# Gates and queries of the mLSTM heads: unscaled turned queries, and gate sums as scans, in a two-layer trunk step

## What is computed

```python
b = jnp.cumsum(fc, -1)
dmat = jnp.where(causal, b[..., :, None] - b[..., None, :] + ic[..., None, :], -jnp.inf)
inter = b + m[..., None]
m_out = jnp.maximum(inter, jnp.max(dmat, -1))
wmat = jnp.exp(dmat - m_out[..., None])
sw = jnp.einsum('bhtd,bhsd->bhts', qc, kc) * wmat
sc_in = jnp.exp(inter - m_out)
num = jnp.einsum('bhts,bhsd->bhtd', sw, vc) + sc_in[..., None] * jnp.einsum('bhvk,bhtk->bhtv', C, qc)
den = jnp.sum(sw, -1) + sc_in * jnp.einsum('bhk,bhtk->bht', n, qc)
h = num / jnp.maximum(jnp.abs(den), jnp.exp(-m_out))[..., None]
```

## Time and profile before

| what | value |
|---|---|
| median of 3 runs | 1513.45 us (1513.32 to 1513.97) |
| the profiled execution's own time | 1512.2 us |
| its span, first to last instruction | 1510.4 us |
| TensorE busy | 1393.6 us (92%) |
| VectorE busy | 622.0 us (41%) |
| ScalarE busy | 338.4 us (22%) |
| GpSimd busy | 340.0 us (23%) |
| mean granted TensorE clock | 0.972 |

### The profile page before, as it was taken

The page is one execution under the profiler, slowest core; times in us unless marked ns, Lnnn a source line. Parts: engine busy times, 40 slices in busy tenths (PEclk is TensorE's granted clock), DMA queues, the critical chain, the costliest instruction groups (busy, mean ns, idle before and its releaser), DMA issues.

```text
span 1510.4 us, 24451 instructions
## 1 busy us (share of the span) xinstructions
PE 1393.6 (92%) x9441; PEld 1071.4 (71%) x9441; DVE 622.0 (41%) x1473; ACT 338.4 (22%) x853; POOL 340.0 (23%) x455
## 2 busy tenths in 40 slices
PE   6999999898998999997899999989899889999964
PEld 5889899675887766564488899976678776656441
DVE  1121435677368312111353124548757852121117
ACT  1211211564101111110142121236431111111102
POOL 0100016632141311111010000744325221212101
PEclk9999999999998999999999999999799999999997
DMA  9420221765817999999732122256461599999984
GB/s 379 142 68 34 94 95 51 255 268 217 335 43 300 371 388 419 418 419 418 302 106 95 67 85 61 94 166 254 193 223 72 197 359 404 420 418 419 418 314 172
DMA packets 79714, 360.60 MB, mean 239 GB/s; under 512 B 20800, under 2 KB 24208, under 8 KB 46064
## 3 DMA queue, kind: packets, MB, share of 16 engines
q1 hardware_dynamic: 43632, 294.76, 49.4%
q0 software_dynamic: 19840, 44.63, 8.3%
q10 hardware_dynamic: 16128, 19.66, 4.1%
HBM read 346.49 MB, written 32.11 MB: 251 GB/s over the span
## 4 chain that ended last, share of the span: by engine, by line
PE 80%; DVE 8%; DMA 6%; issue 3%; ACT 1%; SPq 1%; ACTq 0%; DVEq 0%; POOLq 0%
PE bank L1159 22%; PE bank L1525 16%; PE bank L1396 8%; PE bank L1546 8%; DMA ring<-in_w_exp 4%; PE bank L965 2%; PE bank L1143 2%; PE bank L868 2%; PE bank L1322 2%; PE bank L1506 2%; PE bank L1296 2%; PE bank L1105 1%; PE bank L1418 1%; PE bank L1108 1%; DMA z<-expert_rows 1%
## 5 line engine op out<-in xcount | busy, mean ns | idle before, releaser
L1159 PE MATMUL bank<-ring,hT 128*128 128x256 f32 (+1 forms) x1600 | 338.8, 372 | 1.1 <-DVE z L2264 1.1
L1159 PEld LDWEIGHTS bank<-ring,hT 128*128 128x128 f32 x1600 | 291.9, 191 | 37.7 <-issue 1.6
L1525 PE MATMUL bank<-z,att 128*64 128x256 f32 (+2 forms) x960 | 176.8, 392 | 14.1 <-DMA ring<-in_w_exp 13.7
L1525 PEld LDWEIGHTS bank<-z,att 128*64 128x64 f32 (+2 forms) x960 | 117.3, 150 | 52.5 <-DMA ring<-in_w_exp 14.6
L1396 PE MATMUL bank<-ring,hT 128*128 128x256 f32 x640 | 141.9, 380 | 0.5 <-issue 0.5
L1396 PEld LDWEIGHTS bank<-ring,hT 128*128 128x128 f32 x640 | 120.1, 190 | 16.5 <-issue 0.7
L2717 DVE TENSOR_TENSOR att<-att,bank 128x256 f32<-128x256 f32 x36 | 15.2, 421 | 265.0 <-ACT att L1945 265.0
L3048 POOL DMA_INDIRECT expert_rows<-att,cur x36 | 37.0, 1029 | 354.0 <-DVE att L2730 341.4
L1525 PE MATMUL bank<-ring,att 128*64 128x256 f32 (+2 forms) x672 | 112.7, 398 | 1.8 <-ACT att L1938 1.8
L2264 DVE COPY z<-bank 128x512 f32<-128x512 f32 (+3 forms) x35 | 20.1, 578 | 173.6 <-PE bank L1159 173.6
L1525 PEld LDWEIGHTS bank<-ring,att 128*64 128x64 f32 (+2 forms) x672 | 69.7, 142 | 19.6 <-ACT att L1938 2.2
(11 more groups left out here) (401 smaller groups left out, 2316.7 us busy)
## 6 DMA issues: line engine op xcount, KB each, us to landing
z<-in_w_exp SPq DMA_DIRECT2D x74, 1024.0 KB, 21.9
ring<-in_w_exp SPq DMA_DIRECT2D x72, 1024.0 KB, 19.3
ring<-in_w_ada SPq DMA_DIRECT2D x41, 1024.0 KB, 6.4
ring<-in_w_in SPq DMA_DIRECT2D x24, 1024.0 KB, 5.0
hT<-in_w_exp SPq DMA_DIRECT2D x24, 1024.0 KB, 23.2
att<-in_w_exp SPq DMA_DIRECT2D x12, 1024.0 KB, 19.5
ring<-in_w_out SPq DMA_DIRECT2D x8, 1024.0 KB, 10.5
z<-expert_rows ACTq DMA_DIRECT2D x16, 512.0 KB, 8.6
```

What stands on the lines that cost most here:

```text
L1159: last = eng.matmul(bk[:, i * UN:i * UN + nw], hTv[:, k, t * P:(t + 1) * P], w[:, k, 0:nw], start=(k == 0), stop=(k == KD - 1))
L1525: last = eng.matmul(bank[2 + j][c * m_:(c + 1) * m_, u * DE:(u + 1) * DE], rows, wv[c][k // 4][:, k % 4, :], start=(k == 0), stop=(k == KD ...
```

## The change

TensorE no longer sums the forget gates: it turns input gates and forget gates, two transposes for each tile in place of three matmuls, and VectorE sums the turned rows with two scans for each tile, a backward one over reversed columns. The scaled and turned queries (`qs`, `qts`) are gone, with their transposes, VectorE's scaling and ScalarE's copies. Instead every latent tile keeps its turned, unscaled queries (`qT`, four tiles; tile 0 stays in `qkT`). In `step_values` TensorE writes weights x values to one bank (AN) and queries x state to another (AI), each a group of its own; VectorE multiplies the second with `gs` into `both`, adds the first, and goes on from `both` in SBUF. The job AI was there before (the transposes' bank, opened at g = 0); it is now opened at g = 1 between AN and AU.

```diff
-        a["qs"] = region(att, dead, P, 2, HA, DA)
-        a["qts"] = region(att, dead + 2 * D_A, DA, 2, HA, P)
+        a["qT"] = region(att, dead, DA, NT - 1, HA, P)
+        a["both"] = region(att, dead + (NT - 1) * HA * P, P, HA, W97)
+        turned_q = lambda t: qkT[:, 0] if t == 0 else a["qT"][:, t - 1]
...
-                        eng.matmul(bk[0:36, 0:P], a["gi"][:, t, :], ident, start=True, stop=True)
-                        eng.matmul(bk[0:36, P:2 * P], a["gf"][:, t, :], K["upper"], start=True, stop=False)
-                        last = eng.matmul(bk[0:36, P:2 * P], a["gbk"][:, t, :], K["lower"], start=False, stop=True)
+                        eng.transpose(bk[0:36, 0:P], a["gi"][:, t, :], ident)
+                        last = eng.transpose(bk[0:36, P:2 * P], a["gf"][:, t, :], ident)
...
-                def step_weights(si):
-                    for d, t in STEPS[si] if si > 0 else ():
-                        bk = jobs.open("AI", l, d, t)
-                        eng.wait_ge(*jobs.room())
-                        eng.wait_ge(*ev.at("qs", l, d, t))
-                        for h in range(HA):
-                            last = eng.transpose(bk[0:DA, h * P:(h + 1) * P], a["qs"][:, d, h, :], ident)
-                        last.then_inc(*jobs.filled())
...
-                                              start=True, stop=(t == 0))
-                            if t > 0:
-                                last = eng.matmul(bk[:, h * W97:(h + 1) * W97], a["qts"][:, d, h, :],
-                                                  a["CT"][:, d, h, :], start=False, stop=True)
+                                              start=True, stop=True)
                         last.then_inc(*jobs.filled())
+                        if si > 0:
+                            bk = jobs.open("AI", l, d, t)
+                            eng.wait_ge(*jobs.room())
+                            if si == 1:
+                                eng.wait_ge(*jobs.empty("AS", l, d))
+                                eng.wait_ge(*jobs.empty("AQ", l, t))
+                            else:
+                                eng.wait_ge(*ev.at("CT", l, d, t))
+                            for h in range(HA):
+                                last = eng.matmul(bk[:, h * W97:(h + 1) * W97], turned_q(t)[:, h, :], a["CT"][:, d, h, :],
+                                                  start=True, stop=True)
+                            last.then_inc(*jobs.filled())
...
-                def turned_queries(si):
-                    for d, t in STEPS[si] if si > 0 else ():
-                        bk = jobs.bank("AI", l, d, t)
-                        eng.wait_ge(*jobs.full("AI", l, d, t))
-                        eng.activation(a["qts"][:, d, :, :], bk[0:DA, :].rearrange("p (h n) -> p h n", h=HA),
-                                       ACT.Copy).then_inc(*jobs.freed("AI", l, d, t))
...
+                        for d in range(2):
+                            rows = a["brow"][32 * d:32 * d + HA, t * P:(t + 1) * P]
+                            rows = rows if d == 0 else rows[:, ::-1]
+                            last = eng.tensor_tensor_scan(rows, K["ones"][32 * d:32 * d + HA, 0:P], rows, 0.0, ALU.mult, ALU.add)
+                        last.then_inc(*dve.step())
+                        eng.wait_ge(*dve.last())
...
-                def scaled_queries(si):
-                    eng.wait_ge(*jobs.empty("AE", l))
-                    for d, t in STEPS[si]:
-                        if si > 1:
-                            pd, pt = STEPS[si - 1][d]
-                            eng.wait_ge(*jobs.full("AI", l, pd, pt))
-                        eng.tensor_tensor(a["qs"][:, d, :, :], h4(zv[:, t, C_QA:C_QA + D_A]),
-                                          bc(a["gs"][:, t, 32 * d:32 * d + HA], 2, DA), ALU.mult).then_inc(*dve.event("qs", l, d, t))
...
+                        if si > 0:
+                            state = jobs.bank("AI", l, d, t)
+                            eng.wait_ge(*jobs.full("AI", l, d, t))
+                            eng.wait_ge(*jobs.empty("AE", l))
+                            both = a["both"]
+                            eng.tensor_tensor(both, state[:, 0:HA * W97].rearrange("p (h n) -> p h n", h=HA),
+                                              bc(a["gs"][:, t, 32 * d:32 * d + HA], 2, W97), ALU.mult).then_inc(*jobs.freed("AI", l, d, t))
+                            eng.wait_ge(*jobs.empty("AI", l, d, t))
+                            eng.tensor_tensor(both, both, nv, ALU.add).then_inc(*jobs.freed("AN", l, d, t))
+                            eng.wait_ge(*jobs.empty("AN", l, d, t))
+                            nv = both
```

More of the change, by code:

```diff
@@ L1079, in key_query @@
                     for h in range(HA):
-                        last = eng.matmul(bk[:, h * P:(h + 1) * P], qkT[:, 1, h, :], qkT[:, 0, h, :], start=True, stop=True)
+                        last = eng.matmul(bk[:, h * P:(h + 1) * P], qkT[:, 1, h, :], turned_q(t)[:, h, :], start=True, stop=True)
                     last.then_inc(*jobs.filled())
-                def step_weights(si):
-                    for d, t in STEPS[si] if si > 0 else ():
-                        bk = jobs.open("AI", l, d, t)
-                        eng.wait_ge(*jobs.room())
-                        eng.wait_ge(*ev.at("qs", l, d, t))
-                        for h in range(HA):
-                            last = eng.transpose(bk[0:DA, h * P:(h + 1) * P], a["qs"][:, d, h, :], ident)
-                        last.then_inc(*jobs.filled())
                 def step_values(si):
@@ L1188, in _ @@
                             heads_turned(heads)
-                        if 0 <= idx - STEP0 < len(STEPS) and g == 0:
-                            step_weights(idx - STEP0)
                         if 0 <= idx - STEP0 < len(STEPS) and g == 1:
@@ L1733, in queries_turned @@
                     eng.wait_ge(*jobs.full("AQ", l, t))
-                    eng.activation(qkT[:, 0, :, :], bk[0:DA, :].rearrange("p (h n) -> p h n", h=HA), ACT.Copy).then_inc(*jobs.freed("AQ", l, t))
+                    eng.activation(turned_q(t), bk[0:DA, :].rearrange("p (h n) -> p h n", h=HA), ACT.Copy).then_inc(*jobs.freed("AQ", l, t))
                 def key_query(t):
@@ L1811, in _ @@
                             queries_turned(heads)
-                        if 0 <= idx - STEP0 < len(STEPS) and g == 0:
-                            turned_queries(idx - STEP0)
                         if (idx, g) == (STEP0, 1):
@@ L2115, in gates @@
                                              op0=ALU.min, op1=ALU.subtract)
-                    eng.scalar_tensor_tensor(out=a["gbk"][:, :, 32:36], in0=g1[:, :, 4:8], scalar=0.0,
+                    eng.scalar_tensor_tensor(out=a["gf"][:, :, 32:36], in0=g1[:, :, 4:8], scalar=0.0,
                                              in1=g2[:, :, 4:8], op0=ALU.min, op1=ALU.subtract).then_inc(*dve.event("gates", l))
@@ L2193, in step_weights @@
                         eng.tensor_tensor(a["wt"][:, d, :, :], a["wt"][:, d, :, :], kq[:, t, :, :], ALU.mult).then_inc(*dve.event("sw", l, d, t))
-                    if si < len(STEPS) - 1:
-                        scaled_queries(si + 1)
                 def step_values(si):
@@ L2215, in step_values @@
                         if first:
-                            eng.tensor_tensor(hz, nv[:, :, 0:DA], bc(dn, 2, DA), ALU.mult).then_inc(*jobs.freed("AN", l, d, t))
+                            last = eng.tensor_tensor(hz, nv[:, :, 0:DA], bc(dn, 2, DA), ALU.mult)
+                            last.then_inc(*(jobs.freed("AN", l, d, t) if si == 0 else dve.step()))
                         else:
                             tmp = h4(htmp[:, :])
-                            eng.tensor_tensor(tmp, nv[:, :, 0:DA], bc(dn, 2, DA), ALU.mult).then_inc(*jobs.freed("AN", l, d, t))
-                            eng.wait_ge(*jobs.empty("AN", l, d, t))
+                            last = eng.tensor_tensor(tmp, nv[:, :, 0:DA], bc(dn, 2, DA), ALU.mult)
+                            last.then_inc(*(jobs.freed("AN", l, d, t) if si == 0 else dve.step()))
+                            eng.wait_ge(*(jobs.empty("AN", l, d, t) if si == 0 else dve.last()))
                             eng.tensor_tensor(hz, hz, tmp, ALU.add).then_inc(*dve.step())
@@ L2273, in _ @@
                             keys_turned(heads)
-                        if (idx, g) == (STEP0 - 1, 2):
-                            scaled_queries(1)
                         if 0 <= idx - STEP0 < len(STEPS) and g == 0:
```

6 lines of the change are left out of this document (removed).

## The result

The changed kernel takes 1497.61 us (median, 1497.47 to 1500.41, 4 runs) against 1513.71 us (1513.32 to 1514.82, 4 runs) of the kernel before in the same session: ratio 0.9903, interval 0.9889 to 0.9918, 16.1 us less. In a second session on another occasion it took 1499.51 us (1497.66 to 1502.44, 4 runs) against 1512.36 us (1507.86 to 1516.3, 22 runs): ratio 0.9924, interval 0.9903 to 0.9945, 12.9 us less. The forecast was 11.4 us less and 1502.0 us, with a range of 1497 to 1507.5. The profiled execution of the changed kernel took 1497.47 us with a span of 1495.5, the one of before 1512.2 with 1510.4.

What follows compares the result with a forecast made beforehand. TensorE's records were taken to bound the changed stages: 4.4 us from the gates plus 7.0 from the queries, other terms zero, gave 11.4 us off 1513.45, forecast as 1502.0 us, range 1497 to 1507.5.

Steps and rivals of the forecast that it cites:

- The bound: In the changed stages only the number and size of TensorE's records count; VectorE and ScalarE cost nothing until later than TensorE.
- The list of waits: TensorE's waits: 1.1 us on a PSUM copy in both projection stages, ahead of the gates, next only at the attention's first transposes.
- Part 1, gates on TensorE: Gate sums: 10 records a layer left of 30, saving 2.2 us a layer, 4.4 in both; bounds 2.2 and 2.3 a layer.
- Part 2, scans: Ten added VectorE scans a layer lengthen the gate chain by 2.8 to 5 us, under 8.4 us of cover: cost zero.
- Part 3, the turned queries: Steps 1 to 4: eight TensorE transposes fewer a step, saving 0.87 us a step, 3.5 a layer, 7.0 in both.
- Part 4, two banks: Step values: same matmuls as two groups; taken as zero, bounds -1.8 to +1.8 us for the seams of 16 pairs.
- Part 5, VectorE: Steps: multiplication and addition add 1.1 us a pair on VectorE; 8.2 us of cover left at step 4's weights, cost zero.
- the loads that follow are released by TensorE's own progress, by unit or by bank: Behind the changed stage: later loads are timed by TensorE, so the prediction named no VectorE dependence for them.
- rival (c): Step values to next weights: VectorE becomes the bound, each us beyond the cover costing TensorE one; 1524 at 7 us a pair; chance 0.03.
- the ring of seven: Steps: bank AN is freed at most 0.4 us later and wanted again only after a projection group, so no cost.
- three runs within 0.65 us: Argument from the runs of the kernel before: their small spread speaks against a large clock effect; wandering drops cost little.
- rival (a): Attention: shifted waits change the granted clock, at most 8.6 us a stretch; up to 1510.6 or down to 1493.4; chances 0.10 lost, 0.09 won.

Runs made afterwards that it cites:

- padded: Changed kernel with eight transposes, their results read by nobody, put back on TensorE in each of steps 1 to 4; 1507.72 us, ratio 0.9972 to the kernel before.
- gates_only: Kernel before with only the gate half of the change: two transposes and two scans for each tile, scaled queries kept; 1508.73 us, ratio 0.9977.
- queries_only: Changed kernel with the gate sums turned back to three matmuls a tile and no scans; 1505.19 us, ratio 0.9951 to the kernel before.
- scans_x4: Changed kernel with three further pairs of VectorE scans for each tile, into rows that are written later anyway; 1508.40 us in one run.
- values_plus8: Changed kernel with VectorE's multiplication and addition of each pair with a state done eight times more, 18.9 us more a step; 1587.31 us in one run.
- packed_gates: Changed kernel with both gate sets side by side, turned by one transpose: 5 records a layer instead of 10; 1500.44 us, ratio 0.9918 to the kernel before.

## Why the prediction was right, and where not

**The bound.** Right: fewer TensorE records, less time, at the place of the records. `padded` is the evidence, since it puts back the records alone and 8.2 of the 12.9 us go with them (7.0 in the traces). The list of waits I read with one left out: the stage of layer 1 has a wait of 1.5 us on ScalarE at its very head (757.42 us), far ahead of the change.

**Part 1, gates on TensorE.** Forecast 4.4 us with bounds to 4.6; the trace gives 4.8, `gates_only` 3.6 (interval 1.7 to 5.4). The term is 0.4 too small for both layers: of the 2.41 us a layer, 3.39 - 1.09 = 2.30 lie in the gate records, which is the upper bound that I had and didn't take, and 0.11 in the projection behind them (27.83 us before, 27.72 after). These 0.11 go with the form of the gates, since `queries_only` has 27.82 and `gates_only` 27.72, but I have no cause for them. On fp32 transposes the trace goes on speaking against the Trainium skill's factor of four (TensorE: Matmul & The Clock Gate, Terms): ten of them take 1.09 us, 0.109 each, half of a matmul of two records and not a quarter.

**Part 2, scans.** Cost zero: right. The scans are shorter than the maximum scan I took (409 against 473 ns). The chain up to the exponentials' start had been named wrongly. I let their end move with VectorE; but before the change they stood behind ScalarE's copy out of a projection bank, which TensorE releases, and that came 3.2 us earlier in after. The copy in before and in after, and what follows it in after (ScalarE in order, start us, us):

```profile
91.08 0.38 ACT L1680 ACTIVATE z<-bank 128x256 f32<-128x256 f32 x1 [10.29 <-PE bank L1159]
```

```profile
87.83 0.38 ACT L1672 ACTIVATE z<-bank 128x256 f32<-128x256 f32 x1 [10.06 <-PE bank L1153]
...
91.45 1.28 ACT L1710 ACT_TABLE_LOAD   x1 [3.23 <-DVE att L2137]
92.74 0.74 ACT L1710 ACTIVATE att<-att 36x640 f32<-36x640 f32 x1
```

In after the copy is early enough that the exponentials stand behind VectorE's addition. They end at 94.9 us instead of 97.6, although VectorE's addition at the chain's end (event `mo`) starts 1.4 us later than the 88.36 of the earlier trace rows. Counted from the first gate record the chain has grown by (89.74 - 76.18) - (88.36 - 77.02) = 2.2 us, less than my lower bound of 2.8. Of the kernel after, VectorE's addition and ScalarE's exponentials:

```profile
89.74 0.82 DVE L2137 TENSOR_TENSOR att<-att 36x640 f32<-36x640 f32 x1
```

```profile
93.39 1.55 ACT L1712 ACTIVATE att<-att,small 36x128 f32<-36x128 f32 x5
```

TensorE comes to the columns at 104.99, 10.1 us behind their end, where my working left 3.4 to 5.6. The first transposes need only the exponential of 92.74, so the cover is 11.5; `scans_x4` measured about 11.

**Part 3, the turned queries.** 3.5 us a layer forecast, 3.50 and 3.50 in the trace, and 3.50 lost again in `padded`.

**Part 4, two banks.** 0 forecast, with 1.8 either way. The steps of `padded` and of before agree to 0.01 us in 108.12: the two groups cost nothing.

**Part 5, VectorE.** Both operations 0.56 us, busy 636.1 us (forecast 636). The cover ahead of step 4's weights was 8.2 us in my working. In the trace the first weights are ready at 242.60 + 1.10 = 243.7 and TensorE's values start at 252.17: 8.5.

```profile
233.84 1.10 DVE L2209 TENSOR_TENSOR htmp<-att,small 128x384 f32<-128x384 f32 x1
242.60 1.10 DVE L2173 TENSOR_TENSOR att<-att,ring 128x512 f32<-128x512 f32 x1
...
252.17 1.03 PE L1090 MATMUL bank<-att 128*128 128x97 f32 x8
```

But this part has the failed step of the prediction. It followed VectorE's added time to the next weights, the state and the banks, and stopped at the last step; of what comes next the prediction says that "the loads that follow are released by TensorE's own progress, by unit or by bank". For the loads of the caches that is wrong. Behind that stands a chain that was not named: VectorE's end of the heads, GpSimd's cache loads, TensorE's transposes of the attention. It is the first to break: with 7.1 us more a step the weights were still in time and these loads were not. The change was within its cover (9.1 us left of 11.5), so the sum didn't suffer. The first loss through VectorE can come before the 8.2 us a step that the prediction took for the cover, though once a layer and not once a step as in rival (c). And the bank AN, which I called covered by the ring of seven, is waited for in the same steps as the weights (`values_plus8`, 22.5 us against 19.4). The time beside GpSimd that this part adds to a pair's last multiplication, up to 0.42 us, was 0.54 and 0.07 for the two pairs of step 3 (1.10 and 0.63 us instead of 0.56).

**The clock.** The sentence that failed is that three runs within 0.65 us speak against a large effect. Of 22 runs of before the fastest and the slowest are 8.4 us apart. The drop behind the columns, in one trace of the changed kernel and not in the other, is worth 1.7 us a time. The Trainium skill (TensorE: Matmul & The Clock Gate, Part 1) has the monitor's window run freely and not from the kernel's start; I drew from it that drops would wander, and then let the three runs overrule it. The traces agree with the page: 1.00 and 0.83 at one place of one kernel. The attention, where rival (a) looked, did move its clock, but at a far lower price than 8.6 us. In the 24 us that start 4.3 ahead of layer 1's router sums, as in the earlier trace rows, the granted clock was 0.64 and 0.72 in the two traces of before, 0.64 and 0.79 in those of after and 0.93 in `queries_only`. From the attention's start to the last rows of the router (L1466 before, L1458 after) these five took 201.8, 201.5, 202.0, 201.2 and 199.3 us, 2.7 us between the extremes.

**The total.** 11.4 forecast; 11.8 in the trace at the change's own places; 16.1 and 12.9 between the medians of the two sessions. That the first session's 1497.61 still fell in the range is in part luck: the mechanism accounts for 11.8 of its 16.1 us. Of the 4.3 us between 11.8 and 16.1 the traces hold the 3.0 told above, none of it at an edited instruction, and the rest is how the medians stand to the profiled executions (1.5 us above it before, 0.1 after; I had kept 1.25 for both). All of it is small beside the 8.4 us over which the runs of before spread. The second session's 12.9 has an interval of 8.3 to 14.7 us and so agrees with 11.8; whether some 1 us more belongs to the change, by its shift of the attention for example, stays open.

## What to carry to other kernels

Where one engine is busy without a gap at full clock, count its records by line and multiply by the distance between starts of the same shape: here that gave 3.5 us a layer, and 3.50 was measured. When work moves to another engine, follow its end beyond the stage, to whatever is loaded or overwritten once it is done; the first cover to break may lie behind the last step. And three runs close together don't bound the spread of a kernel: measure the halves of a change in one session, with many runs of the kernel before.

## What the runs showed of the hardware

- An fp32 transpose of 128 moving columns costs 0.11 us from start to start, with 36 columns turned (ten in 1.09 us, after) and with 100 (five in 0.55 us, `packed_gates`).
- The granted clock can differ at one place between two executions of one kernel, with TensorE fully busy in both: 1.00 and 0.83 in the same 10 us. In `scans_x4` two short waits (1.36 and 0.68 us) were followed by 32 records at 10.19 us instead of 7.17. That the waits did it is likely but not shown, because the drop also comes without them.
- A VectorE operation with two SBUF operands took 1.10 us at 233.84 us, while GpSimd was computing beside it, and 0.56 at 255.98 us, where GpSimd computed nothing (both L2209; the mean of its eight is 714 ns). At 239.23 us, with GpSimd computing too, it took 0.63, so not each meeting costs as much. The two new operations with a PSUM operand took 0.55 to 0.56 us in both places.
